# Five edits to a three-layer forward pass in split fp32: u's pairs issued by ScalarE, the leads' second sum moved ahead, the last quarter of each lead's residual made by GpSimd, a new order in flip chunks and the first chunk

## The reference

```python
x = x + rmsnorm(mix, post_mix_g[layer])
f = sq_relu_mlp(rmsnorm(x, pre_mlp_g[layer]), mlp_w1[layer], mlp_w2[layer])
x = x + rmsnorm(f, post_mlp_g[layer])
```

## Time and profile before

| | us |
|---|---|
| median of 3 runs | 3159.99 (3158.95 to 3161.25) |
| the profiled execution's own time | 3159.14 |
| its span (first to last instruction) | 3157.3 |
| PE busy | 3136.6 |
| DVE busy | 1911.5 |
| ACT busy | 1555.8 |
| POOL busy | 259.3 |

### The profile page before, as it was taken

How to read it: one execution, slowest core, us unless ns; L and a number is a source line. 1 busy time by engine, 2 the same in 40 slices (tenths; PEclk the granted TensorE clock), 3 DMA queues, 4 the chain that set the end, 5 groups by cost and what they waited for, 6 DMA issues and landing times.

```text
span 3157.3 us, 39011 instructions
## 1 busy us (share of the span) xinstructions
PE 3136.6 (99%) x15644; PEld 2622.1 (83%) x15644; DVE 1911.5 (61%) x2140; ACT 1555.8 (49%) x2123; POOL 259.3 (8%) x329
## 2 busy tenths in 40 slices
PE   9999999999999999999999999999999999999999
PEld 8777888888888888888888888878888888888887
DVE  5677655555555768665564655668976544445445
ACT  6655543434444569564443434554455443444344
POOL 0000000000000020000820006720000000000000
PEclk9999999999999999999999999999999999999999
DMA  7555666666666555665666666766655666666664
GB/s 237 145 150 166 187 191 189 191 194 187 193 188 205 165 189 187 213 182 187 194 190 192 188 194 224 247 215 207 207 159 169 199 190 194 188 187 196 189 195 154
DMA packets 329317, 601.73 MB, mean 191 GB/s; under 512 B 33792, under 2 KB 44976, under 8 KB 329136
## 3 DMA queue, kind: packets, MB, share of 16 engines
q1 hardware_dynamic: 326064, 593.91, 60.8%
q10 hardware_dynamic: 3072, 5.33, 0.6%
HBM read 587.09 MB, written 11.01 MB: 189 GB/s over the span
## 4 chain that ended last, share of the span: by engine, by line
PE 96%; DVE 2%; ACT 2%; issue 0%; DMA 0%; SPq 0%; ACTq 0%; DVEq 0%
PE pair L2155 24%; PE pair L2157 24%; PE pair L2156 24%; PE pair L2293 6%; PE misc_ps L2293 3%; PE pair L2298 3%; PE turn_ps L2293 3%; PE misc_ps L2298 2%; PE turn_ps L2298 1%; PE turn_ps L2186 1%; ACT hi L670 1%; PE pair L2452 1%; DVE lo L1331 1%; PE pair L2559 1%; PE misc_ps L2467 0%
## 5 line engine op out<-in xcount | busy, mean ns | idle before, releaser
L1331 DVE TENSOR_TENSOR lo<-raw,hi 128x1024 fp32r<-128x1024 f32 x1084 | 1342.6, 1247 | 843.9 <-ACT hi L670 835.4
L670 ACT ACTIVATE hi<-raw 128x1024 fp32r<-128x1024 f32 x1084 | 1139.0, 1058 | 1101.5 <-PE pair L2157 824.9
L2155 PE MATMUL pair<-hi,xt_hl 128*128 128x512 f32 (+1 forms) x1952 | 770.5, 395 | 3.9 <-DVE lo L1331 2.9
L2157 PE MATMUL pair<-lo,xt_hl 128*128 128x512 f32 (+1 forms) x1952 | 757.6, 388 | 0.0
L2156 PE MATMUL pair<-hi,xt_hl 128*128 128x512 f32 (+1 forms) x1952 | 756.8, 388 | 0.0
L2155 PE MATMUL pair<-hi,ht_h 128*128 128x512 f32 x1504 | 586.6, 390 | 0.0
L2157 PE MATMUL pair<-lo,ht_h 128*128 128x512 f32 x1504 | 585.3, 389 | 0.0
L2156 PE MATMUL pair<-hi,ht_l 128*128 128x512 f32 x1504 | 585.2, 389 | 0.0
L2155 PEld LDWEIGHTS pair<-hi,xt_hl 128*128 128x128 f32 x1952 | 366.7, 188 | 87.4 <-issue 7.0
L2157 PEld LDWEIGHTS pair<-lo,xt_hl 128*128 128x128 f32 x1952 | 366.5, 188 | 76.4
L2156 PEld LDWEIGHTS pair<-hi,xt_hl 128*128 128x128 f32 x1952 | 367.0, 188 | 70.9
(11 more groups left out here) (343 smaller groups left out, 2299.0 us busy)
## 6 DMA issues: line engine op xcount, KB each, us to landing
raw<-in_mlp_w SPq DMA_DIRECT2D x512, 512.0 KB, 4.1
raw<-in_w_gate SPq DMA_DIRECT2D x88, 512.0 KB, 4.3
raw<-in_w_up SPq DMA_DIRECT2D x88, 512.0 KB, 4.1
raw<-in_w_down SPq DMA_DIRECT2D x88, 512.0 KB, 4.6
raw<-in_even_w_in SPq DMA_DIRECT2D x68, 512.0 KB, 4.0
raw<-in_odd_w_in SPq DMA_DIRECT2D x64, 512.0 KB, 3.7
raw<-in_w_in SPq DMA_DIRECT2D x64, 512.0 KB, 4.2
raw<-in_even_w_out SPq DMA_DIRECT2D x32, 512.0 KB, 4.1
```

What stands on the lines that cost most here:

```text
L670: nc.scalar.activation(hi[:, r], raw[:, slot], ACT.Copy).then_inc(sems["hi_ready"], 1)
L1331: nc.vector.tensor_tensor(lo[:, r], raw[:, slot], hi[:, r].bitcast(F32), ALU.subtract).then_inc(sems["lo_ready"], 1)
L2155: nc.tensor.matmul(to, xh[:, t0 + k, tok], h[:, k], start=s, stop=False)
L2157: mm = nc.tensor.matmul(to, xh[:, t0 + k, tok], l[:, k], start=False, stop=e)
```

## The change

1. **u's pairs.** The four DMAs are issued by ACT (`pair_up`) and no longer by SP: for the first four groups right behind the copy of u, for the other four at slot 33 behind waits. `drive(0)` stands at slot 14 and no longer at slot 13.
2. **The second sum.** In a post lead DVE's `sum_squares(1)` stands ahead of `tile_lo(lead, 1, 0)`, and ACT's `tile_root(1)` ahead of a `conv`.
3. **The last quarter.** DVE's two `residual(3, m)` are gone; POOL makes them in two instructions each.
4. **Flip chunks.** In the first unit (j = 0) all matmuls of banks 0 and 1, hi and lo, come first, then those of banks 2 and 3.
5. **The first chunk** of the kernel takes its first unit for both token tiles before the second unit (`head` 1 for 2).
6. **The end.** One of eight output DMAs is issued by ACT. Also SP's program is recorded first of the five.

```diff
 class Scalar
+    if to[0] == "halves" and not self.paired:
+        self.eng.wait_ge(sems["split_done"], T.at("split_done", -1))
+        self.pair_up(0)
...
+    if slot == 33:
+        self.eng.wait_ge(sems["bu_ready"], 4)
+        self.eng.wait_ge(sems["split_done"], self.T.at("split_done"))
+        self.pair_up(1)
...
     self.tile_hi(lead, 1, 0)
+    self.tile_root(1)
     self.conv()
-    self.tile_root(1)
...
 class Vector
+    self.sum_squares(1)
     self.tile_lo(lead, 1, 0)
-    self.sum_squares(1)
     self.tile_factor(1)
...
     self.tile_gain(1)
-    self.residual(3, 0)
-    self.residual(3, 1)
+    T.add("x_ready", 2)
     self.convs(2)
     self.late_lo(lead, 3)
...
 class Tensor
-    head = 4 if post or units == 4 and tail else 2
+    head = 4 if post or units == 4 and tail else 1 if lead and lead.kind == "first" else 2
...
+    for part in ((0, 1), (2, 3)) if j == 0 else ((0, 1, 2, 3),):
...
-    if g is not None:
+    if g:
         self.drive(g)
+    if slot == BU + 1:
+        self.drive(0)
...
 class Pool
     if lead and lead.kind == "post":
-        self.eng.wait_ge(sems["x_ready"], T.add("x_ready", len(TILES)))
+        T.add("x_ready", len(TILES))
+        T.add("gain_used", 4)
+        self.eng.wait_ge(sems["x_ready"], T.at("x_ready", 2))
+        self.eng.wait_ge(sems["gain_used"], T.at("gain_used"))
+        for m in range(M):
+            x = xres[:, m, 3 * CH:4 * CH]
+            part = acc[:, m, 3 * CH:4 * CH] if m else tmp[:, 0]
+            self.ts(part, part, st(RPOST + m), None, ALU.mult)
+            nc.gpsimd.tensor_tensor(x, part, x, ALU.add).then_inc(sems["x_ready"], 1)
+        self.eng.wait_ge(sems["x_ready"], T.at("x_ready"))
```

More of the change, by code:

```diff
@@ L355, in build @@
         Y_ORDER = (1, 0, 2, 3)
-        u_split = []
         def s5_step(slot, after):
@@ L563, in load_b @@
                                            scratch_b[g, 32 * j:32 * j + 32, kinds]).then_inc(sems["b_loaded"], 16)
[L565 to L574, removed]
             def load_c(self, g):
@@ L599, in mix_at @@
                         self.eng.dma_start(mask[:, k], i["consts"][:, a:a + SEQ]).then_inc(sems["masks_loaded"], 16)
-                if slot in (21, 43):
-                    self.load_u(int(slot == 43))
                 g = s5_step(slot, 12)
@@ L627, in final @@
                     for who, n in (("out_ready_act", 0), ("out_ready_dve", 3), ("out_ready_act", 1), ("out_ready_dve", 2)):
+                        if (m, n) == (1, 1):
+                            continue
                         self.eng.wait_ge(sems[who], self.T.add(who))
@@ L748, in split @@
                     a.then_inc(sems["split_done"], 1)
-                    if to[0] == "halves":
-                        u_split.append(T.at("split_done", -1))
+                    if to[0] == "halves" and not self.paired:
+                        self.eng.wait_ge(sems["split_done"], T.at("split_done", -1))
+                        self.pair_up(0)
                 elif to[0] is not None:
@@ L755, in split, with pair_up @@
                 T.add("split_done")
+            paired = 0
+            def pair_up(self, c):
+                for token in range(2):
+                    for h in range(2):
+                        nc.scalar.dma_start(u_pair[64 * token:64 * token + 64, :, h],
+                                            u2[64 * h:64 * h + 64, 4 * c:4 * c + 4, token * HALF:token * HALF + HALF]
+                                            ).then_inc(sems["u_paired"], 16)
+                self.paired += 1
             def split_conv(self, to):
@@ L1299, in final @@
                         nc.scalar.activation(y, y, ACT.Copy, scale=st(RS + m)).then_inc(sems["out_ready_act"], 1)
+                self.eng.wait_ge(sems["out_ready_act"], 4)
+                nc.scalar.dma_start(out_v[:, 1, CH:2 * CH], acc[:, 1, CH:2 * CH]).then_inc(sems["stored"], 16)
         class Vector(Program):
@@ L2286, in flip_chunk @@
                     h, l = (w[:, r].rearrange("p (t n) -> p t n", t=KU) for w in (hi, lo))
[L2287 to L2298, removed]
+                    for part in ((0, 1), (2, 3)) if j == 0 else ((0, 1, 2, 3),):
+                        for k in range(KU):
+                            t, s = KU * j + k, j == 0 and k == 0
+                            for f in part:
+                                if s and f >= 2 and n % 2 == 0:
+                                    self.own_half_free(f - 2)
+                                ps, cols = self.BANKS[n % 2][f // 2][:, f % 2], slice(f * P, (f + 1) * P)
+                                nc.tensor.matmul(ps, h[:, k, cols], xt_hl[:, t].rearrange("p two s -> p (two s)"), start=s,
+                                                 stop=False)
+                        for k in range(KU):
+                            t, e = KU * j + k, j == units - 1 and k == KU - 1
+                            for f in part:
+                                ps, cols = self.BANKS[n % 2][f // 2][:, f % 2], slice(f * P, (f + 1) * P)
+                                a = nc.tensor.matmul(ps[:, 0:SEQ], l[:, k, cols], x[0][:, t], start=False, stop=e)
                     a.then_inc(sems["unit_used"], 1)
@@ L2968, in build, with _ @@
         block = ctx.enter_context(nc.Block())
+        @block.sync
+        def _(sp):
+            model(Sync(sp))
         @block.scalar
@@ L2984, in _ @@
             model(Pool(pool))
-        @block.sync
-        def _(sp):
-            model(Sync(sp))
 def shape_constants():
```

## The result

The changed kernel takes 3180.32 us (median of 4 runs, 3178.70 to 3180.46), the kernel before 3160.62 beside it: 1.0061 times as long, 95% interval 1.0048 to 1.0075, 19.7 us more. The profiled execution took 3178.70 us, its span is 3176.9, 19.6 above the span before.

A forecast was written before the change was run, and what follows sets the result against it. PE's own instruction stream was taken as the bound, so only its idle time counts. Stalls 19.4 plus clock 6.0 less gains 11.2 gave +14.2 us on 3159.14, 3173.3; it predicted 3173.5, range 3164 to 3181.

The forecast's parts named there:

- own range: Range of the forecast itself, 3168 to 3180 us, from the product's price, the clock and drive(1); chance 0.60.
- What would show it: Signs: four PE waits for GpSimd of 4 to 5 us, stretched `lo`, no u wait; wrong if the clock holds.
- Start: First chunk: PE makes tile 1 of unit 0 while idle before unit 1's `lo`; gain 1.1 us.
- Flip chunks: Flip chunks' starts: matmuls on banks 0 and 1 first remove five PE waits, 0.85 us or up to twice; gain 1.2.
- Second sum: Post leads: sum and root made earlier move the residual and `lo` up; gain 0.6 us four times, 2.4.
- u's pairs: At drive(0): earlier issue and later drive remove PE's 5.23 us wait and 1.54 of low clock; gain 6.0 after a charge.
- charge of 0.8: At drive(1): PE, now sooner, was expected to wait for `b_w`; 0.8 us taken off the gain.
- u's pairs are late on ACT's queue: Rival at drive(0): transfers landing over 10 us after issue make PE wait again; 3178 us, chance 0.07.
- End: Last four outputs: one issue moved to ACT's queue; gain 0.45 us.
- The last quarter: Before quarter 3's turn: POOL's chain of 6.35 us makes PE wait 4.85 us in each of four leads, 19.4.
- I take 0.7: Assumed price in us of POOL's product by a column, likened to a copy; ends 0.61 and 1.29.
- The clock: Behind the four last-quarter stalls: lower granted clock costs 1.5 us each, 6.0 in all (ends 0 and 8).

The follow-up runs named there:

- u_act: The kernel before with only the issue of u's pairs moved to ACT, drive(0) staying at slot 13: 3158.61 us, ratio 0.9995.
- drive_late: The kernel before with only drive(0) one slot later, SP still issuing u's pairs: 3152.74 us, ratio 0.9976.
- dve_quarter: The changed kernel with the last quarter's residual given back to VectorE, everything else of the change kept: 3146.68 us, ratio 0.9956 to the kernel before.
- early_one_lo: The changed kernel with POOL making tile 0's half early and one of DVE's two `lo` put behind its wait for POOL's last sum: 3160.59 us.
- lo_behind: The changed kernel with DVE waiting for POOL's second sum before its two `lo` behind the gain: 3171.92 us, ratio 1.0035 to the kernel before.
- pool_only: The kernel before with only the last quarter's residual moved to POOL: 3194.01 us, ratio 1.0105.

## Why the prediction was right, and where it was off

It forecast 3173.5 us, slower; 3180.3 lies inside the range of 3164 to 3181, 6.8 above the forecast and 0.7 below the upper edge. The "own range" of 3168 to 3180, from the bounds of the terms, was just left, so a little luck was in it. The mechanism of the largest step was right: PE waits for GpSimd ahead of the turn of quarter 3 in all four leads, and the clock falls behind each. Of the signs under "What would show it" two were off: the waits are 6.2 to 6.3 us and not 4 to 5, and DVE's two `lo` did not stretch; POOL's product did.

**Start** 1.1: 1.3. **Flip chunks** 1.2: 1.7, the "about twice that" which it had allowed for 0.85 of idle time. **Second sum** 2.4: 2.4. Each was read from the idle times of the earlier trace rows and was there.

**u's pairs** 6.0: 6.9 by the trace. The 6.8 of stall and clock came whole, and the charge of 0.8 for a new wait at drive(1) was wrong: there is none. What the prediction put first, that ACT issues sooner, contributes almost nothing (u_act); "`drive(0)` now follows unit 15" does it alone (drive_late). The rival "u's pairs are late on ACT's queue" showed in two profiled executions of kernels with ACT's issue: in dve_quarter a landing of 11.2 us and a wait of 1.1, in early_one_lo 11.1 and 0.9. In the changed kernel PE has 1.6 us to spare.

**End** 0.45: 0 by the trace; all that was gained is there at the last matmul already. SP's last issue stands 0.5 us sooner behind it, but that transfer took 0.5 us longer to land.

**The last quarter** 19.4: 25.7 (four stalls of 6.45). This term was mis-sized, and in one step: "I take 0.7", the product by a column. The copy of the earlier trace rows, to which it was likened, takes 0.61; the product takes 1.56, beyond the upper end of 1.29. The chain is 1.6 us longer: 0.73 by the first product (1.43 us behind the second `lo`), 0.86 by the second, 0.12 by the two sums, less 0.1 of steps. Why a product by a column takes more than a sum no run here shows. But the trace before had a hint that the copy was the wrong likeness. With no instruction of DVE beside it, POOL's instruction by a constant of 128x32 takes 0.29 us, one of two such tiles mostly 0.24 to 0.27, and a copy 0.21 to 0.25:

```profile
1404.02 0.29 POOL L2664 TENSOR_SCALAR s<-s 128x32 f32<-128x32 f32 x1
1404.39 0.26 POOL L2660 TENSOR_TENSOR s<-s 128x32 f32<-128x32 f32 x1
```

The order was wrong but not its share: `lo`, product, `lo` was forecast, the two `lo` came first and then the product; both put two `lo` (2.3 us) into the chain. The order came from the earlier trace rows, where POOL and DVE did take turns. There POOL's instructions were sums, here a product; whether that is what decides, no run here shows. lo_behind takes the two `lo` out and shortens each stall by 1.9 us.

The Trainium skill's "SBUF — State Buffer" ("SBUF: two separate sides") says that a VectorE instruction with two SBUF inputs and a GpSimd instruction that reads SBUF take a shared port pair by an exclusive lock for a whole instruction, and that whichever starts first gets it. That the loser stands still and isn't only slowed agrees with the 1.57, 2.36 and 3.42 us beside none, one and two `lo`, which read `raw` and `hi`. Who comes next differs, if the start of a record is when an instruction asks for the pair: POOL's product was there at 357.03, before the second `lo` began, and that `lo` went ahead of it.

By the Trainium skill's "GPSIMD Engine Reference" (3.1 Elementwise) the product would be 0.44 us and the sum 1.11, an estimate from its cycles. The sum's 1.26 is near it; the product's 1.56 is three and a half times as long, and the measurement decides. The same page of the Trainium skill (4.1 Engine selection) keeps elementwise work on VectorE. The traces agree: two instructions of GpSimd, 2.8 us together, stand for one of VectorE of 0.75.

**The clock** 6.0: 6.4, from 1.2 to 2.0 in a lead. That the sum is so near has some luck in it: pool_only, with stalls as long, lost 8.5. "What would show it" named a hold of the clock as a way to be wrong; it did not hold, and early_one_lo shows that at a stall of 2.5 us it might have.

**The sum**: 25.7 + 6.4 - 12.5 = 19.6 us, where 12.5 is 1.3 + 1.7 + 2.4 + 6.9 and a remainder of 0.2.

## What to carry to other kernels

An operation between the last sum of a stage and the next stage's first matmul is paid in full beyond the little that TensorE still has to do (1.5 us here): give it to the engine that does it in fewest and shortest instructions, however busy that engine is elsewhere. Before work goes to GpSimd, look for that operation with that kind of operand in a trace, and count what VectorE has queued beside it. When a wait for a transfer goes after an edit of two parts, run each alone: here, by the traces, the later use was worth 6.7 us and the sooner issue 0.5, and the kernel that keeps the quarter on VectorE with the rest of the change (3146.7 us) beats both kernels.

## What was unexpected of the hardware

- A product of 128x512 by a column takes GpSimd 1.56 us, more than its sum of two such tiles (1.26) and its copy (0.61).
- GpSimd's product waits for the whole run of VectorE's back-to-back `lo`: 1.57, 2.36 and 3.42 us with none, one and two.
- Stalls of 3.5, 4.5 and 6.4 us each brought the lower clock and cost 1.1 to 2.5 us behind them, by how much of it fell on work; one of 2.5 us did in one lead of four, one of 1.7 in none.
- Of four transfers issued 2.65 us sooner (u_act) the last landed only 1.8 sooner.
